# A convolutional FFN on Trainium2: its up projection moves from plain matmuls to Strassen products, and its 3x3 convolution from padded copies to PSUM

## The reference, cut to what matters

```python
def conv_ffn(h, w_up, conv_w, conv_b, w_down, rows):      # h: 512 tokens x 1024
    u = h @ w_up                                           # 1024 -> 5632 channels
    u = conv2d_grid(u, conv_w, rows) + conv_b              # depthwise 3x3 on an 8 x 64 grid of tokens
    gate, val = jnp.split(u, 2, axis=-1)                   # 2816 channels each
    return (jax.nn.silu(gate) * val) @ w_down              # 2816 -> 1024
...
x = x + g2 * conv_ffn(modulate(rms_norm_2(x, norm2_g), sh2, sc2), ...)
return rms_norm_2(x, final_g)
```

## Time and profile before

| | us |
|---|---|
| three executions | 1918.32, 1921.46, 1922.24 |
| profiled execution, its own time | 1916.31 |
| its span in the trace | 1914.5 |
| PE busy | 1811.7 (95% of the span) |
| DVE busy | 960.1 (50%) |
| ACT busy | 502.0 (26%) |
| POOL busy | 306.4 (16%) |

### The profile page before, as it was taken

The page is one execution under the profiler, slowest core; times in us unless marked ns, Lnnn a source line. Parts: engine busy times, 40 slices in busy tenths (PEclk is TensorE's granted clock), DMA queues, the critical chain, the costliest instruction groups (busy, mean ns, idle before and its releaser), DMA issues.

```text
span 1914.5 us, 35490 instructions
## 1 busy us (share of the span) xinstructions
PE 1811.7 (95%) x14918; PEld 1202.8 (63%) x14918; DVE 960.1 (50%) x1920; ACT 502.0 (26%) x1056; POOL 306.4 (16%) x372
## 2 busy tenths in 40 slices
PE   7999999999999999999999979888898999998997
PEld 3445675588888888743555468888643444444886
DVE  3560442334444423233231577666615899899433
ACT  4021562211111100134112644444403222221001
POOL 1150011101111100011000074554010011101100
PEclk9999997999999999999999989999999999998999
DMA  6521101343343334432312000000121222221232
GB/s 214 177 73 48 56 2 55 119 167 119 123 132 111 121 132 133 131 121 75 125 55 72 23 3 5 4 5 4 52 77 58 76 76 76 77 77 55 88 99 77
DMA packets 43595, 157.89 MB, mean 82 GB/s; under 512 B 4984, under 2 KB 5640, under 8 KB 42424
## 3 DMA queue, kind: packets, MB, share of 16 engines
q1 hardware_dynamic: 37152, 132.14, 21.5%
q10 hardware_dynamic: 6296, 23.58, 3.3%
HBM read 150.96 MB, written 6.31 MB: 82 GB/s over the span
## 4 chain that ended last, share of the span: by engine, by line
PE 75%; DVE 10%; issue 9%; ACT 3%; DVEq 1%; DMA 0%; POOL 0%; SPq 0%; ACTq 0%; POOLq 0%
PE psum L364 21%; PE psum L1382 14%; PE psum L1557 13%; PE psum L1242 6%; DVE mem L2908 4%; PE psum L2313 2%; PE psum L2317 2%; PE psum L1029 2%; DVE mem L2503 1%; PE psum L622 1%; PE psum L1010 1%; PE psum L1191 1%; PE psum L997 1%; PE psum L2079 1%; DVE mem L2916 1%
## 5 line engine op out<-in xcount | busy, mean ns | idle before, releaser
L364 PE MATMUL psum<-mem 128*128 128x512 f32 (+1 forms) x1568 | 652.1, 576 | 17.9 <-DMA mem<-in_units 10.8
L364 PEld LDWEIGHTS psum<-mem 128*128 128x128 f32 x1568 | 297.6, 191 | 361.1 <-issue 342.2
L1557 PE MATMUL psum<-mem 128*128 128x256 f32 x1232 | 274.3, 383 | 11.7 <-DVE mem L1297 11.7
L1382 PE MATMUL psum<-mem 128*128 128x256 f32 x1232 | 274.2, 382 | 2.5 <-issue 2.5
L1557 PEld LDWEIGHTS psum<-mem 128*128 128x128 f32 x1232 | 234.5, 191 | 49.3 <-DVE mem L1297 12.5
L1382 PEld LDWEIGHTS psum<-mem 128*128 128x128 f32 x1232 | 232.1, 190 | 40.5 <-issue 7.6
L2908 DVE SCALAR_TENSOR_TENSOR mem<-mem 128x512 f32<-128x512 f32 x352 | 239.3, 755 | 0.0
L1242 PE MATMUL psum<-mem 128*128 128x512 f32 x256 | 114.1, 606 | 3.1 <-DVEq L2825 1.9
L1309 POOL TENSOR_TENSOR mem<-mem 128x256 f32<-128x256 f32 x22 | 16.4, 745 | 582.3 <-DVE mem L2916 308.2
L1242 PEld LDWEIGHTS psum<-mem 128*128 128x128 f32 x256 | 49.2, 194 | 67.4 <-issue 62.1
L419 POOL TENSOR_TENSOR mem<-mem 128x512 f32<-128x512 f32 x24 | 30.4, 1266 | 367.9 <-ACT mem L403 367.6
(11 more groups left out here) (383 smaller groups left out, 2112.5 us busy)
## 6 DMA issues: line engine op xcount, KB each, us to landing
mem<-in_units SPq DMA_DIRECT2D x246, 512.0 KB, 3.6
mem<-in_cw ACTq DMA_DIRECT2D x2, 2048.0 KB, 10.9
mem<-in_wn ACTq DMA_DIRECT2D x1, 2048.0 KB, 9.2
bias_tiles<-bias_scratch ACTq DMA_DIRECT2D x1, 2048.0 KB
mem<-bias_tiles ACTq DMA_DIRECT2D x1, 2048.0 KB
mem<-in_xT ACTq DMA_DIRECT2D x1, 2048.0 KB, 9.5
x_scratch<-mem ACTq DMA_DIRECT2D x1, 2048.0 KB, 8.9
mem<-x_scratch ACTq DMA_DIRECT2D x1, 2048.0 KB, 7.7
```

Of the source, the lines that this page charges most:

```text
L364: last = pe.matmul(dst, w[:, k, :], rhs(k), start=(k == 0), stop=(k == 7))
L1382: last = eng.matmul(dst, w[:, k, :], rhs(k), start=start and k == 0, stop=stop and k == 3, skip_group_check=True)
L1557: ins = eng.matmul(dst, w[:, k, :], rhs(k0 + k), start=opens and first and k == 0, stop=closes and last_ and k == k1 - k0 - 1, skip_group_ ...
```

## The change: what it does

Tile 0 stays as it was on PE: two full products. From tile 1 on, the two units of a tile (W1 for the gate side, W2 for the value side) and the two halves of the tokens (256 each, `lo` and `hi`) form a 2 x 2 block product, done in seven half-size products instead of eight: 28 matmuls of 128x128 by 128x256 per tile, where before 16 of 128x512 stood. The seven results land in banks y (0 to 2), z (3 to 5) and x (6, 7) by `n % 3` and `n % 2`; between the products ACT saves four partial results to SBUF (`keep`: head, five, mid, tail), and DVE puts the missing quarters together and writes them back to PSUM (`quarters`, three tensor_tensor of 256 columns per tile). The differences of tokens are made once by DVE (`tokens`, 16 tensor_tensor of 256 columns). The sums of weights (four tensor_tensor of 512 columns per tile) are made by GpSimd, into wsum2, with two buffers.

The padded grid and its copies go. ACT makes the centre tap (`centre`) from PSUM into the accumulator, two activations of 512 columns per tile; DVE adds the eight other taps straight from PSUM, each cut at the grid's edge (7x63, 8x63 or 7x64 elements instead of 8x64). One gate multiply per tile stays on DVE, and one SiLU on ACT. The loops are unrolled.

`ffn2` and `down2` get the ring of 6 slots; the two further slots (ring3) lie where the scan's data was, so SP waits for the end of that stage (`stage_done`, 8) before ffn2's first unit. down2's sums of chunks 0 and 1 are made by GpSimd (`ahead=2`), those of the later chunks by DVE as before; down2's banks are 1, 4, 7, 6 instead of 4, 5, 7, 6, with a wait for tile 19's convolution before its first product and one for the last tile's second quarter before bank 7 is written.

```diff
-WIDE = ("ffn1", "down1", "pleproj", "ple")
+WIDE = ("ffn1", "down1", "pleproj", "ple", "ffn2", "down2")
...
-            return ring[:, SLOT[n]] if SLOT[n] < NSLOTS else ring2[:, SLOT[n] - NSLOTS]
+            if SLOT[n] < NSLOTS:
+                return ring[:, SLOT[n]]
+            return (ring2 if n < UNIT0["ffn2"] else ring3)[:, SLOT[n] - NSLOTS]
...
+                    if j == 0 and third:
+                        third(eng)
...
+                    if j + 1 < ahead:
+                        continue
+                    if j + 1 == ahead > 1:
+                        eng.wait_ge(summed, s0 + 4 * ahead)
...
+        hX2 = hX[:2] + [r11.take(4, CTX)]
+        cacc = r11.take(2, 2, 8, 64)
+        csil = r11.take(S)
+        parts2 = [r11.take(CTX) for _ in range(3)]
+        r11.at = gcen.offset + 4 * S
         wsum2 = r11.take(2, 4, 4, P)
-        down2_work = [r11.take(CTX) for _ in range(3)]
+        ring3 = r11.take(NWIDE - NSLOTS, 8, P)
...
-                linear_pe(eng, u0, 2 * FT, lambda k: hT[:, k, 0:S], free, ready=ready)
...
+                unit_landed(eng, u0)
+                product(eng, held(u0), lambda k: hT[:, k, 0:S], bank_z(0), ready).then_inc(units_done, 1)
+                unit_landed(eng, u0 + 1)
+                product(eng, held(u0 + 1), lambda k: hT[:, k, 0:S], bank_y(0)).then_inc(units_done, 1)
+                for n in range(1, FT):
+                    u, y, z, ws = u0 + 2 * n, bank_y(n), bank_z(n), wsum2[:, n % 2]
+                    summed = s0 + 4 * (n - 1)
+                    unit_landed(eng, u)
+                    if n >= 3:
+                        eng.wait_ge(convolved, 2 * (n - 3) + 2)
+                    half(y[:, lo], held(u), lambda k: hT[:, k, lo], stop=False).then_inc(made, 1)
+                    eng.wait_ge(f1_sums, summed + 1)
+                    eng.wait_ge(hX_put, hx0 + 4)
+                    half(z[:, hi], ws[:, 0], lambda k: hX2[0][:, k, :], stop=False).then_inc(made, 1)
+                    eng.wait_ge(f1_sums, summed + 3)
+                    eng.wait_ge(hX_put, hx0 + 8)
+                    eng.wait_ge(kept, 4 * (n - 1) + 1)
+                    half(y[:, lo], ws[:, 1], lambda k: hX2[1][:, k, :], start=False, stop=False).then_inc(made, 1)
+                    if n >= 3:
+                        eng.wait_ge(taken, 3 * (n - 3) + 2)
+                    half(bank_x(n), held(u)[:, 4:8], lambda k: hT[:, 4 + k, lo]).then_inc(made, 1)
+                    eng.wait_ge(f1_sums, summed + 4)
+                    eng.wait_ge(hX_put, hx0 + 16)
+                    eng.wait_ge(kept, 4 * (n - 1) + 3)
+                    half(y[:, lo], ws[:, 2], lambda k: hT[:, k, hi], start=False, stop=False).then_inc(units_done, 1)
+                    half(z[:, hi], ws[:, 3], lambda k: hT[:, 4 + k, hi], start=False).then_inc(made, 1)
+                    unit_landed(eng, u + 1)
+                    eng.wait_ge(kept, 4 * (n - 1) + 4)
+                    half(y[:, lo], held(u + 1)[:, 4:8], lambda k: hX2[2][:, k, :], start=False).then_inc(units_done, 1)
...
+                def centre(n):
+                    for side, bank in ((0, bank_z(n)), (1, bank_y(n))):
+                        if n == 0:
+                            eng.wait_ge(units_done, u0 + side + 1)
+                        else:
+                            eng.wait_ge(taken, 3 * (n - 1) + 2 + side)
+                        if n >= 2:
+                            eng.wait_ge(gated, n - 1)
+                        eng.activation(cacc[:, n % 2, side].rearrange("p y x -> p (y x)"), bank, ACT.Copy,
+                                       scale=fcw[:, 4, n + FT * side:n + FT * side + 1]).then_inc(centred, 1)
...
+                    eng.wait_ge(made, after("11", n))
+                    keep(head2, bank_y(n)[:, lo], n)
+                    centre(n - 1)
+                    eng.wait_ge(made, after("s1", n))
+                    keep(five2, bank_z(n)[:, hi], n)
+                    if n >= 2:
+                        silu(n - 2)
+                    eng.wait_ge(made, after("s2", n))
+                    keep(mid2, bank_y(n)[:, lo], n)
+                    eng.wait_ge(units_done, u0 + 2 * n + 1)
+                    keep(tail2, bank_y(n)[:, lo], n)
+                centre(FT - 1)
+                silu(FT - 2)
+                silu(FT - 1)
...
+                def tokens():
+                    for q in range(4):
+                        ready(eng, q)
+                        eng.tensor_tensor(hX2[0][:, q, :], hT[:, q, hi], hT[:, q, lo], ALU.subtract).then_inc(hX_put, 1)
...
+                    eng.wait_ge(units_done, u0 + 2)
+                    for q in range(4):
+                        eng.tensor_tensor(hT[:, q, hi], hT[:, 4 + q, hi], hT[:, q, hi], ALU.subtract).then_inc(hX_put, 1)
...
+                def quarters(n):
+                    y, z = bank_y(n), bank_z(n)
+                    eng.wait_ge(kept, 4 * (n - 1) + 3)
+                    eng.wait_ge(made, after("s4", n))
+                    eng.tensor_tensor(z[:, hi], z[:, hi], mid2[n % 2], ALU.add).then_inc(taken, 1)
+                    eng.tensor_tensor(z[:, lo], bank_x(n), head2[n % 2], ALU.add).then_inc(taken, 1)
+                    eng.wait_ge(kept, 4 * (n - 1) + 4)
+                    eng.wait_ge(units_done, u0 + 2 * n + 2)
+                    eng.tensor_tensor(y[:, hi], five2[n % 2], tail2[n % 2], ALU.add).then_inc(taken, 1)
+
+                def gate(n):
+                    eng.wait_ge(convolved, 2 * n + 2)
+                    eng.wait_ge(silued, n + 1)
+                    eng.scalar_tensor_tensor(act2T[:, n, :], cacc[:, n % 2, 1].rearrange("p y x -> p (y x)"),
+                                             fcb[:, FT + n:FT + n + 1], csil, ALU.add, ALU.mult).then_inc(gated, 1)
...
+                    taps = [tap for tap in range(9) if tap != 4]
+                    for t, tap in enumerate(taps):
+                        dy, dx = tap // 3 - 1, tap % 3 - 1
+                        to = (slice(None), slice(max(0, -dy), 8 - max(0, dy)), slice(max(0, -dx), 64 - max(0, dx)))
+                        of = (slice(None), slice(max(0, dy), 8 + min(0, dy)), slice(max(0, dx), 64 + min(0, dx)))
+                        for side, bank in ((0, bank_z(n)), (1, bank_y(n))):
+                            acc = cacc[:, n % 2, side][to]
+                            src = bank.rearrange("p (y x) -> p y x", y=8)[of]
+                            w = fcw[:, tap, n + FT * side:n + FT * side + 1]
+
+                            def add():
+                                return eng.scalar_tensor_tensor(acc, src, w, acc, ALU.mult, ALU.add)
...
+                tokens()
+                for n in range(FT):
+                    between = {}
+                    if n:
+                        between[2] = lambda: gate(n - 1)
+                    if n + 1 < FT:
+                        between[5] = lambda: quarters(n + 1)
+                    convolve(n, between)
+                gate(FT - 1)
...
+                    lay_weights(eng, f1_sums, s0 + 4 * (n - 1), held(u), held(u + 1), wsum2[:, n % 2], 4)
+                    lay_last_weights(eng, f1_sums, s0 + 4 * (n - 1), held(u), wsum2[:, n % 2], 4)
+                    if n >= 5 and n % 2:
+                        products((n - 5) // 2)
+                for j in range(2):
+                    eng.wait_ge(made, after("s4", FT - 2 + j))
+                    down2_first[0](eng, j)
+                for i in range(HALF - 2, HALF):
+                    products(i)
...
+            def before(eng):
+                eng.wait_ge(sem("f2_convolved"), 2 * (FT - 3) + 2)
+
+            def third(eng):
+                eng.wait_ge(sem("f2_taken"), 3 * (FT - 2) + 2)
+
             pe, dve, copy, source, weights = paired_residual(
                 "down2", 2, lambda k: act2T[:, 2 * k, :], lambda k: act2T[:, 2 * k + 1, :], act2X, 4 * HALF, wsum2, down2_work,
-                (4, 5, 7, 6), gate=lambda m: mod[:, 40 + m, 0:1])
-            down2_first.append(lambda eng: weights(eng, 0))
+                (1, 4, 7, 6), before=before, gate=lambda m: mod[:, 40 + m, 0:1], ahead=2, third=third)
+            down2_first.append(weights)
...
+                if n == UNIT0["ffn2"]:
+                    eng.wait_ge(stage_done, 8)
```

128 lines of the change are left out of this document (62 added, 66 removed).

## The result

The changed kernel takes 1868.6 us (median of four runs, 1866.9 to 1873.4), the kernel before beside it 1919.9 us (1915.5 to 1922.2): a ratio of 0.974, 95% interval 0.9713 to 0.9766. The forecast was 1878 in a range of 1869 to 1898: the measured median stands at the range's lower edge, 0.4 us beyond it as the numbers are written. The gain is 51 us between the medians, and 43 were forecast. The profiled execution took 1868.32 us, its span is 1866.5. Against the 1916.31 us of the execution shown before, that is 48.0 us less, and two views say where they are.

The account below looks back on a forecast made before the run. PE's matmuls were taken to bound ffn2, with DVE's lateness paid at the border to down2. The terms -30.2 - 14.2 + 1.0 = -43.4 us gave 1872.9 for the profiled execution, 1878 from the median, range 1869 to 1898.

Parts of the forecast that it names:

- PE sets the pace, and the products pay in full: In ffn2, PE stays the bound and 21 tiles with fewer products take 30.2 us less.
- A Strassen tile costs 12.30 us: PE's time for a 56-record tile in ffn2, read from an ffn1 tile, against 13.74 us before.
- halving the columns does not quite halve the record: PE's 256-column records against 512-column ones: 7 products for 8 give 10.5% and not 12.5%.
- Rival D: Whole kernel: nothing collides or waits, the start is free and some unbooked old waits go: 1873 us, chance 0.07.
- The border gives 14.2 us: From ffn2 to down2, PE's waits and the slow records behind them go: 14.2 us less.
- GpSimd's last differences would end 19 us into down2: At down2's start, GpSimd finishes chunk 2's differences at E + 19, before PE wants them at E + 24.6.
- DVE's tile of 11.9 us, port waits 0.5: In ffn2, DVE's work of 11.4 us per tile plus 0.5 of waits beside GpSimd stays under PE's 12.30.
- Rival A: In ffn2's convolution, taps from PSUM don't overlap, pitch 0.69 instead of 0.605 us: 1897 us, chance 0.13 before mixtures.
- Rival B: In ffn2, gate multiply and third quarter both wait for GpSimd's sums, 2.1 us per tile: 1901 us, chance 0.11 before mixtures.
- Rival C: In ffn2, DVE's taps collide with GpSimd through their SBUF accumulator: 1970 us, slower than before, chance 0.05.
- The start, 1.0 us: Ahead of ffn2, GpSimd's sums for tile 2 collide with DVE's scaling of the norm: 1.0 us more (0 to 3).
- From the execution to the median: Whole kernel: 5.2 us added because the old profiled execution lay that far under the median of its runs.

Follow-up runs that it names:

- plain_products: The changed kernel with ffn2's Strassen products taken back to full ones, convolution and border as changed: 1899.5 us, ratio 0.9902 to the kernel before.
- sums_on_dve: The changed kernel with ffn2's sums of weights made by DVE instead of GpSimd: 1898.5 us, ratio 0.9896 to the kernel before.
- border_on_dve: The changed kernel with down2's sums of chunks 0 and 1 back on DVE: 1873.9 us, ratio 0.976 to the kernel before.
- sums_shifted: The changed kernel with GpSimd starting a tile's sums after the first product of the tile before: 1866.4 us, ratio 0.9712 to the kernel before.
- taps_from_sbuf: The changed kernel with the taps reading their source from SBUF (hT) instead of PSUM: 1942.2 us, ratio 1.0111 to the kernel before.

## Why the prediction came out as it did

- **PE sets the pace, and the products pay in full.** Right. PE has no wait in 387.6 us; plain_products gives back the 34.4 us of ffn2 and leaves down2 as it is.
- **A Strassen tile costs 12.30 us.** The step that was mis-sized. The 12.30 came from a tile of ffn1 with other work on both sides; inside it the records follow each other every 0.216 us as everywhere, but the first takes 0.32 us to the next start and the last 0.31, and these two ends are the 0.19 us too much. A tile with a wait ahead of it lasts 12.35 us from first start to last end here too (sums_on_dve). In an unbroken run it is 12.11: 21 x (13.74 - 12.11) = 34.2 us, where 30.2 were booked. With it goes the remark that halving the columns does not quite halve the record: 0.2162 us (12.11 / 56) against 0.4294 is nearly half, and 7 for 8 gives 11.9%, not 10.5. Rival D, in which nothing collides or waits, used the same price, and so its 1873 lies 4 us above the measurement. The prediction even had a second row that seemed to confirm the figure, 119.56 us for 544 records, but these begin right behind a wait. The kernel before, in windows:

```profile
1780.00:1785.00 5.00, 4.97 (x15) 4.10 (x16) 3.06 (x5) 0.00 (x0) 0.56 (x1) 0.66 0.00 0
...
1790.00:1890.00 100.00, 100.00 (x464) 87.38 (x464) 35.21 (x69) 4.57 (x9) 6.34 (x5) 1.00 0.28 90
```

  The first five microseconds hold 15 records at a granted clock of 0.66, a later hundred touches 464 at full clock: with the 0.38 us that one record lasts, (100 + 0.38) / 464 = 0.2163 us from start to start. The changed kernel has the same 464 in 100 us, in ffn2 and in down2. The better price stood in the trace of the kernel before.
- **The border gives 14.2 us.** Right in mechanism, 2.1 short: down2's 616 records cost 133.3 and not 135.4, for the same reason. The waits of before cost more than their length: 11.7 us of idle time and 4.6 of slow records. Two things share the gain, as border_on_dve shows: some 10 us go with the lighter convolution, 6 with GpSimd's sums. That GpSimd's last differences would end 19 us into down2 was met: down2 begins at 1717.35, the last difference ends 19.05 us later, and PE, which wants it 112 records or 24.2 us behind that start, does not wait. GpSimd's timeline:

```profile
1735.36 1.04 POOL L1316 TENSOR_TENSOR mem<-mem 128x256 f32<-128x256 f32 x1
```

- **DVE's tile of 11.9 us, port waits 0.5.** Right in size: 11.4 of work; the sixteen taps 9.65 us, 0.603 each, against 0.605; a quarter at 0.33 against 0.32. The wait for GpSimd is 0.7, always at L2999, as the prediction placed it. It foresaw idle time of DVE before L2999 as well. There is hardly any: the wait inside L2999 fills DVE's spare time, and sums_shifted, which takes it away, shows 0.5 us of idle time per tile in its place.
- **Rival A (taps from PSUM at their full duration).** Out, by the pitch of 0.59. The rule of the Trainium skill (page "VectorE: DVE Perf Modes", section "The TRN2 errata") that was weighed beside it, 120 cycles with a PSUM operand against 58, is not met: the same taps have a median of 668 ns from PSUM and 678 from SBUF (L3019 in taps_from_sbuf). By that rule, as the prediction worked it out, 17 us of the gain would have gone; they did not.
- **Rival B (both port waits).** Half of it is there, one wait of 0.7 us per tile and not two of 1.06. PE pays nothing.
- **Rival C (taps collide).** Not here, and real as soon as the source is SBUF.
- **The start, 1.0 us.** PE's idle time ahead of ffn2 is 4.99 us instead of 4.45, so 0.5 us. DVE's eight multiplies take 7.61 us instead of 5.39, but PE begins with the first of them, and tile 0 then takes no longer than before: 15.66 us for 32 records, 1.9 over their price, where it was 2.1.
- **What was not in the prediction:** 1.7 us more at out2 (50.98 us for the 114 records that took 49.3 before) and 0.9 more at the end, where nothing is changed. Both go with a lower granted clock behind a wait: 0.85 instead of 1.00 from 1390 to 1400, and 0.60 instead of 0.76 at the end. Over the kernels here, which all have the same out2, the stretch from 1390 to 1400 was granted anything from 0.67 to 1.00, so I count it as scatter of single executions. Without these 2.6 us the sum would have been 7 us off and not 4.6; that they hid a part of the error is luck.
- **From the execution to the median.** 5.2 us were added because the profiled execution of before lay that far under its median. That was not a property of the kernel: the one of after lies 0.3 under its median. By the sum alone the forecast was 1872.9, 4.6 above the execution measured; these 5.2 us are more than half of the 9.4 by which 1878 is too high.
